# Router logits from un-normalised features, a first gather in pieces, another order of expert groups, and a second layer norm by column blocks

## The reference

```python
h = layer_norm(DEEPNORM_ALPHA * x + merged @ w_o, ln1_g, ln1_b)
# hierarchical_moe(h): top-1 of 4 groups, then top-2 of its 8 experts
grp_logits = tok @ w_gr + b_gr
exp_logits = (tok @ w_er + b_er).reshape(-1, N_GROUPS, EXPERTS_PER_GROUP)
...
hid = silu(tok @ w_g[e]) * (tok @ w_u[e])      # 32 experts, 2048 -> 256 -> 2048
out = (hid * combine) @ w_d[e]
ple = sigmoid(h @ w_pg) * (p @ w_pp)           # w_pg 2048 x 2048, w_pp 256 x 2048
x_new = layer_norm(DEEPNORM_ALPHA * h + moe + ple, ln2_g, ln2_b)
```

## Time and profile before

| | us |
|---|---|
| median of 3 runs (lowest, highest) | 1623.52 (1616.81, 1628.93) |
| the profiled execution, its time | 1617.29 |
| the profiled execution, its span | 1615.5 |
| busy: PE, PEld, DVE, ACT, POOL | 1435.6, 1082.9, 758.8, 333.8, 96.9 |
| moved by DMA, mean rate | 353.23 MB, 219 GB/s |

### The profile page before, as it was taken

How to read it: one execution, slowest core, us unless ns; L and a number is a source line. 1 busy time by engine, 2 the same in 40 slices (tenths; PEclk the granted TensorE clock), 3 DMA queues, 4 the chain that set the end, 5 groups by cost and what they waited for, 6 DMA issues and landing times.

```text
span 1615.5 us, 21195 instructions
## 1 busy us (share of the span) xinstructions
PE 1435.6 (89%) x8725; PEld 1082.9 (67%) x8725; DVE 758.8 (47%) x1499; ACT 333.8 (21%) x468; POOL 96.9 (6%) x94
## 2 busy tenths in 40 slices
PE   6969999999999999998999989888999698789671
PEld 4968998777788678768999975563465265346220
DVE  3749777888864246315565554302213142120237
ACT  3413331000010010015344442131202101200102
POOL 2730000000010100000010020000000000000002
PEclk9979999999999799979999996799999899999976
DMA  8424444333333433424554470389999999999991
GB/s 220 151 92 164 142 148 133 109 109 109 108 121 118 130 100 110 136 98 137 180 188 169 170 295 27 137 337 359 392 405 409 409 403 372 409 406 405 409 380 55
DMA packets 139039, 353.23 MB, mean 219 GB/s; under 512 B 20644, under 2 KB 21724, under 8 KB 138416
## 3 DMA queue, kind: packets, MB, share of 16 engines
q1 hardware_dynamic: 135944, 341.99, 57.8%
q0 software_dynamic: 2992, 9.81, 2.1%
HBM read 344.60 MB, written 7.18 MB: 218 GB/s over the span
## 4 chain that ended last, share of the span: by engine, by line
PE 75%; DMA 12%; DVE 7%; issue 2%; ACT 2%; SPq 1%; DVEq 0%; ACTq 0%
PE bank L520 72%; DMA mslot<-in_w_exp_up 6%; DMA mslot<-in_w_exp_down 5%; DVE lo L1574 1%; DVE atok L2327 1%; ACT hi L1303 1%; PE bank L535 1%; PE bank L792 1%; DMA stS<-in_state_hgrn 1%; SPq L1158 1%; DMA ident<-in_consts 1%; ACT htok L1422 0%; DVE stS L1896 0%; DVE stats L2408 0%; PE bank L907 0%
## 5 line engine op out<-in xcount | busy, mean ns | idle before, releaser
L520 PE MATMUL bank<-XT,raw 128*128 128x264 f32 x1280 | 309.1, 402 | 0.0
L520 PEld LDWEIGHTS bank<-XT,raw 128*128 128x128 f32 x1280 | 250.3, 198 | 47.3 <-issue 3.2
L1574 DVE TENSOR_TENSOR lo<-raw,hi 128x2048 fp32r<-128x2048 f32 x68 | 157.3, 2314 | 132.7 <-ACT hi L1303 132.6
L520 PE MATMUL bank<-mslot,Xg 128*32 128x512 f32 (+1 forms) x1024 | 146.6, 664 | 41.1 <-DMA mslot<-in_w_exp_up 40.0
L1303 ACT ACTIVATE hi<-raw 128x2048 fp32r<-128x2048 f32 x68 | 130.1, 1914 | 233.3 <-PE bank L520 229.8
L520 PE MATMUL bank<-XH,hi 128*128 128x264 f32 x512 | 148.9, 291 | 7.4 <-DVE lo L1574 6.2
L520 PE MATMUL bank<-XL,hi 128*128 128x264 f32 x512 | 147.3, 288 | 0.0
L520 PE MATMUL bank<-XH,lo 128*128 128x264 f32 x512 | 146.3, 286 | 0.0
L520 PEld LDWEIGHTS bank<-mslot,Xg 128*32 128x32 f32 (+1 forms) x1024 | 40.6, 123 | 124.5 <-issue 123.6
L520 PE MATMUL bank<-HT,mslot 128*128 128x264 f32 x512 | 116.3, 387 | 0.0
L520 PE MATMUL bank<-mslot,hidT 128*32 128x512 f32 (+1 forms) x512 | 79.6, 719 | 33.2 <-DMA mslot<-in_w_exp_down 33.2
(11 more groups left out here) (389 smaller groups left out, 2268.4 us busy)
## 6 DMA issues: line engine op xcount, KB each, us to landing
raw<-in_w_in SPq DMA_DIRECT2D x72, 1024.0 KB, 5.1
mslot<-in_w_exp_gate SPq DMA_DIRECT2D x128, 512.0 KB, 11.2
mslot<-in_w_exp_up SPq DMA_DIRECT2D x128, 512.0 KB, 12.8
mslot<-in_w_exp_down SPq DMA_DIRECT2D x64, 1024.0 KB, 14.0
raw<-in_w_out SPq DMA_DIRECT2D x16, 1024.0 KB, 5.0
mslot<-in_w_ple_gate SPq DMA_DIRECT2D x16, 1024.0 KB, 14.3
raw<-in_w_branch_b SPq DMA_DIRECT2D x8, 1024.0 KB, 5.0
raw<-in_w_branch_a SPq DMA_DIRECT2D x8, 1024.0 KB, 5.0
```

The costliest lines, as they stand in the source:

```text
L520: return nc.tensor.matmul(out, w, x, start=start, stop=stop)
L1574: v.tensor_tensor(lo[:, n % RD, :], raw[:, n % RD, :], hi[:, s % RH, :].bitcast(F32), ALU.subtract).then_inc(lo_done, 1)
```

## The change

- **Router.** `wrr` is loaded with feature k*128+p on partition p (before p*16+k). Its gain is multiplied in while the last dense product runs (at `N_O`, on DVE), and `raw_logits` multiplies it with the un-normalised `XT`, four tiles after each `to_tokens`. Scale and shift are applied to the 36 logits per token, with the column sums `wall`. `h_features` and `logits` go.
- **First gather.** It takes `htok` itself in float32 (three products per tile instead of five split ones) and stands in pieces ahead of the first three steps of the first group (`FIRST_GATHER`). The two slices of the gate product ahead of the selection go, so all ten slots are loaded with expert weights; the split of `htok` comes after the first gather.
- **HT** is made from `XT` by DVE and ACT during the first two groups, with the scalars spread over partitions by PE (`spread_scalars`).
- **Plan.** Fixed group, four quads, two pairs, two quads; the gate product moves to groups 2, 3, 4 and 7, `rest` to group 8. Feature order of the gate weights as for `wrr`.
- **Second layer norm.** Statistics of a column block follow its scatter in the last group; gain and bias come as two 8 KB loads which `norm_rows` spreads with eight products on PE; final scaling writes `ynorm` in halves of 1024 columns, and the stores stand ahead of the test of `flag`. The last group's down weights come in three pieces of 2, 1 and 1 column blocks (`pieces`).

The reading of the flag and the jump have left their place behind the last adding, and the statistics of a block follow its adding, two rows a block. The diff, cut to its core:

```diff
-PLANS = [[list(range(FIXED))] + PAIRS[2:4] + QUADS] + [PAIRS] * 4
+PLANS = [[list(range(FIXED))] + QUADS[:4] + PAIRS[2:4] + QUADS[4:]] + [PAIRS] * 4
...
-PLE_AT = {0: 0, 3: 1, 5: 2, 7: 3}
-PLE_AHEAD = (0, 1)
-REST_AT = 5
+PLE_AT = {2: 0, 3: 1, 4: 2, 7: 3}
+REST_AT = 8
+FIRST_GATHER = {0: (0, 1, 2), 1: (3, 4), 2: (5, 6, 7), 3: ()}
...
+        def pieces(rnd, g):
+            return ((0, 2), (2, 3), (3, 4)) if (rnd, g) == (0, len(PLANS[0]) - 1) else ((0, 2), (2, 4))
...
+            def raw_logits(j):
+                if j == 0:
+                    pe.wait_ge(w_gained, 1)
+                    b = side("wall")
+                    mm(b[:, 0:72], ones[:, :], wsum[:, :, :].rearrange("p i n -> p (i n)"), True, True).then_inc(
+                        misc_ready, 1)
+                for J in range(4 * j, 4 * j + 4):
+                    last = mm(bank[7][0:36, 0:NT], wrr[:, J], XT[:, J], J == 0, J == KD - 1)
+                if j == 3:
+                    last.then_inc(logT_done, 1)
...
+                    raw_logits(j)
...
-            def h_features(k):
-                b = side(("ht", k))
...
+                if cb == 0 and kq == 0:
+                    pe.wait_ge(ht_done, KD)
...
-            for kq in PLE_AHEAD:
-                ple_gate(0, kq)
...
+            def first_gather(u):
+                b = side(("ga", 0, 0, u))
+                if u == 0:
+                    pe.wait_ge(norm_act, 3)
+                    pe.wait_ge(zeroed, 3)
+                    pe.wait_ge(sel_ready, 1)
+                sel = [selm[:, 0, 0, 0:128].bitcast(F32), selm[:, 0, 1, 0:128].bitcast(F32),
+                       sels[0:NB, 0, 0:128].bitcast(F32)]
+                for q in range(2):
+                    ks = slice((2 * u + q) * 128, (2 * u + q + 1) * 128)
+                    for tt, (t0, tn) in enumerate(TOK):
+                        last = mm(b[:, q * 256:q * 256 + 128], htok[0:tn, tt, ks], sel[tt], tt == 0, tt == 2)
+                last.then_inc(misc_ready, 1)
...
+            def spread_scalars():
+                pe.wait_ge(diag_ready, 1)
+                for i in range(2):
+                    b = side(("spread", i))
+                    for tt, (t0, tn) in enumerate(TOK):
+                        last = mm(b[:, t0:t0 + tn], ones[0:tn, :], diag[0:tn, i, t0:t0 + tn], True, True)
+                    last.then_inc(misc_ready, 1)
...
+                        for u in FIRST_GATHER[s]:
+                            first_gather(u)
+                        stored(("ga", 0, 0, 2 * s))
+                        stored(("ga", 0, 0, 2 * s + 1))
                     for i in range(ne):
...
                     turn(rnd, g)
+                if rnd == 0:
+                    norm_rows(0)
                 for nb in range(4):
                     scatter(rnd, groups - 2, nb)
...
+            def norm_rows(again):
+                pe.wait_ge(ln2_ld, 32)
+                for r in range(8):
+                    b = side(("row", again, r))
+                    mm(b[:, :], ident[0:8, r:r + 1].to_broadcast([8, 128]), ln2row[:, :], True, True).then_inc(
+                        misc_ready, 1)
...
-                                 t["w_ple_gate"][0].rearrange("(p k) n -> p k n", p=P)[
+                                 t["w_ple_gate"][0].rearrange("(k p) n -> p k n", p=P)[
...
+                            dst = mslot[c % RM][:, 0:1024 * (n1 - n0)]
+                            sp.dma_start(dst.rearrange("p (j d) -> p j d", j=2),
+                                         src[:, :, 512 * n0:512 * n1]).then_inc(m_land[c % RM], 16)
...
+                    if rnd == 0 and g == len(plan) - 1:
+                        sp.wait_ge(misc_ready, misc["ple", 3, 2][0] + 1)
+                        for i, n in enumerate(("ln2_gain", "ln2_bias")):
+                            sp.dma_start(ln2row[4 * i:4 * i + 4, :], t[n][0].rearrange("(r n) -> r n", r=4)).then_inc(
+                                ln2_ld, 16)
...
-                gate_up_done(sp, rnd, len(plan) - 1)
-                for i, n in enumerate(("ln2_gain", "ln2_bias")):
-                    sp.dma_start(ln2[:, i, :], t[n].to_broadcast([P, D])).then_inc(ln2_ld, 16)
-            ple_load(0, PLE_AHEAD)
...
+            def store_rows(again):
+                for tt, (t0, tn) in enumerate(TOK):
+                    dst = outs[0][0, t0:t0 + tn, :] if tt < 2 else outs[1].rearrange("b a d -> (b a) d")
+                    for half in range(2 if tt < 2 else 1):
+                        cs = slice(1024 * half, 1024 * (half + 1)) if tt < 2 else slice(0, D)
+                        if tt < 2 or again:
+                            sp.wait_ge(f_out, 4 * again + 2 * tt + half + 1 + (tt == 2))
+                        else:
+                            sp.wait_ge(f_small, 1)
...
+                pool.dma_start(wrr[:, :, 4:36],
+                               t["w_expert_router"][0].rearrange("(k p) g -> p k g", p=P)).then_inc(r_ld, 16)
...
+            pool.wait_ge(flag_ready, 1)
             for tt in range(3):
                 nc.gpsimd.memset(atok[:, tt, :], 0.0).then_inc(zeroed, 1)
...
+                        nc.scalar.activation(htok[0:tn, tt, :], htok[0:tn, tt, :], ACT.Identity,
+                                             bias=nmr[0:tn, tt:tt + 1],
                                              scale=rstd[0:tn, tt:tt + 1]).then_inc(norm_act, 1)
-            act.wait_ge(norm_dve, 1)
...
+            def norm_rows(again):
+                for r in range(8):
+                    b, read = side(("row", again, r))
+                    if r == 0:
+                        gate_up_done(act, *((4, len(PLANS[4]) - 1) if again else (0, len(PLANS[0]) - 1)))
+                    nc.scalar.activation(ln2[:, r // 4, (r % 4) * 512:(r % 4 + 1) * 512], b[:, :],
+                                         ACT.Copy).then_inc(read, 1)
...
                 for tt, (t0, tn) in enumerate(TOK):
-                    last = v.tensor_tensor(logit[0:tn, tt, :], b[0:tn, tt * 36:(tt + 1) * 36],
-                                           rbias[0:tn, :], ALU.add)
+                    link(v.scalar_tensor_tensor(out=logit[0:tn, tt, :], in0=wall[0:tn, 0, :],
+                                                scalar=nmr[0:tn, tt:tt + 1], in1=wall[0:tn, 1, :],
+                                                op0=ALU.mult, op1=ALU.add))
+                settle()
+                for tt, (t0, tn) in enumerate(TOK):
+                    last = v.scalar_tensor_tensor(out=logit[0:tn, tt, :], in0=b[0:tn, tt * 36:(tt + 1) * 36],
+                                                  scalar=rstd[0:tn, tt:tt + 1], in1=logit[0:tn, tt, :],
+                                                  op0=ALU.mult, op1=ALU.add)
                     if tt < 2:
                         link(last)
...
+                                         lnk[:, 1, :].unsqueeze(2).to_broadcast([P, KD, 36]), ALU.mult))
+                    settle()
+                    link(v.tensor_tensor(wrr[:, :, :], wrr[:, :, :],
+                                         lnk[:, 0, :].unsqueeze(2).to_broadcast([P, KD, 36]), ALU.mult))
+                    link(v.tensor_reduce(wsum[:, 1, :], wrb[:, :, :].rearrange("p k n -> p n k"), AX_X, ALU.add))
+                    settle()
+                    v.tensor_reduce(wsum[:, 0, :], wrr[:, :, :].rearrange("p k n -> p n k"), AX_X,
+                                    ALU.add).then_inc(w_gained, 1)
...
+                for i, scalar in enumerate((rstd, nmr)):
+                    for tt, (t0, tn) in enumerate(TOK):
+                        last = v.tensor_scalar(diag[0:tn, i, t0:t0 + tn], ident[0:tn, 0:tn], scalar[0:tn, tt:tt + 1],
+                                               None, ALU.mult)
+                last.then_inc(diag_ready, 1)
...
+            def h_lows():
+                dve.wait_ge(h_high, 3)
+                dve.wait_ge(misc_ready, misc["ga", 0, 0, 7][0] + 1)
+                v.tensor_tensor(hS[32:32 + NB], by_k(htok[0:NB, 2, :]), hS[0:NB].bitcast(F32),
+                                ALU.subtract).then_inc(split_done, 1)
+                for half in range(2):
+                    for tt in range(2):
+                        h_low(tt, half)
...
+            def features():
+                for i in range(2):
+                    side_read(dve, ("spread", i))
+                for half in range(2):
+                    x = XT[:, 8 * half:8 * half + 8, :]
+                    for i, op in enumerate((ALU.mult, ALU.add)):
+                        if i:
+                            dve.wait_ge(ht_mul, 2 * half + 1)
+                        v.tensor_tensor(x, x, spread_ln[:, i, :].unsqueeze(1).to_broadcast([P, 8, NT]),
+                                        op).then_inc(ht_mul, 1)
...
+            def row_statistics(nb):
+                for tt, (t0, tn) in enumerate(TOK):
+                    final_link(v.bn_stats(stats[0:tn, tt, nb, :], atok[0:tn, tt, nb * 512:(nb + 1) * 512]))
+            def last_give_back(g):
+                store(0, g, 0)
```

(35 more changed lines are left out.)

314 lines of the change are left out of this document (150 added, 164 removed).

## The result

The changed kernel takes 1609.8 us (median of 10 runs, 1602.66 to 1611.91), the kernel before in the same comparison 1622.8 us (10 runs, 1616.81 to 1628.93). The ratio is 0.9914, with a 95% interval of 0.9894 to 0.9934: 13 us faster, where 31.5 were forecast. The profiled execution took 1610.45 us with a span of 1608.6.

The account below looks back on a forecast made before the run. Weight DMA (210 MB) was taken to bound the time after the router, with the queue idle in the router. 41.4 - 2.8 - 15.4 = 23.2 us to the last landing plus 8.3 in the tail: 31.5 off 1623.5 gives 1592 us, range 1573 to 1609.

Parts of the forecast that it names:

- Tail: From the last landing to the end: 45.65 us shrinks to 37.3, 8.3 us won, bounds 5 and 12.
- Dense stage: Twelve raw-logit products among the dense blocks, partly in PE's idle time: +3.5 us, bounds 0 and 7.
- the ring: Dense stage: ring of three banks instead of four makes PE wait about 1 us in the first round.
- Router: First four slots come free at 990 us, 46.5 us earlier; net 41.4 with ten slots loaded instead of twelve.
- The stream: Expert and embedding weight loads after the router: loses 22.2 us against 19.4 before, 2.8 us given back.
- The hand walk: Both plans walked group by group, PE pieces 3% above rows, 2.56 us a slot: last landings 1563.4 before, 1524.8 new.
- They are balanced: Groups 2, 3 and 4, each with an embedding part: 73, 64 and 73 us of PE against 73 of DMA.
- Ahead of the last landing: Last two half-size down loads wait for slots the first down piece frees: 15.4 us given back, bounds 5 and 19.
- Rival 2: PE bounds the stream; at 8% instead of 3% the landing comes 17 us later: 1609 us (1602 to 1616), chance 0.15.
- Rival 1: Clock stays up and PE keeps ahead; landing 15 us earlier: 1576 us (1569 to 1583), chance 0.24.
- Rival 3: Slower than before: PE waits for weights, its clock drops, stacked groups start at the lower level: 1633 us, chance 0.04.
- Rival 4: Router step not early: ACT's queue or the smaller ring delays the first copies 15 to 20 us: 1610 us, chance 0.07.

Follow-up runs that it names:

- Run 1: Changed kernel with the 8-row tile's last gain and bias step done by DVE instead of ACT and POOL: 1602.88 us, ratio 0.9885.
- run 4: Changed kernel with all sixteen products of raw logits behind the dense stage's last transposes, none between its blocks: 1606.93 us, ratio 0.9909.
- run 2: Changed kernel with the last group's down weights in two halves again (8 loads, not 12): 1603.35 us, ratio 0.9882.
- run 3: Changed kernel with gain and bias rows spread by two DMA copies instead of PE's products and ACT's copies: 1599.43 us, ratio 0.9862.
- run 5: Changed kernel with two units of the first gather, not three, ahead of the first gate/up step: 1606.62 us, ratio 0.9895.
- all together: Changed kernel plus small tile on DVE, gain/bias rows by DMA, first down piece before scatter 7, two units first, embedding part in group 1: 1583.9 us, ratio 0.9751.

## Why the prediction was wrong, point by point

The sign was right and so was most of the mechanism, but one of the two gains, the tail's, did not come at all. The size was 2.4 times too large: 13 us instead of 31.5, and 1609.8 lies just outside the range, which ended at 1609. From MH: 31.5 forecast, minus 5.9 in the router, minus 4.7 in the stream and ahead of the landing, minus 9.8 in the tail, is 11.1.

- **Tail (forecast +8.3, bounds 5 and 12; measured -1.5). This is the step that failed**: "DVE's eight halves at 2.29 / 2 = 1.15 to 1.2 us", beside "two rows of 4.5 on POOL". The durations were nearly right (1.27, 4.70), but they were laid side by side, and the two engines exclude each other. DVE lost 10.87 - 2.44 = 8.4 us, and its other halves took 0.4 us more than forecast. Another 1.6 us are DVE's row after the landing, with the scalars ready 22.9 us behind it instead of 21.3. From DVE's last instruction to the end are 6.0 us, where the forecast had 6.5 (37.3 - 30.8). That is 9.8 to 9.9 in all. Nor was POOL's small tile last, as forecast: it was done at 1596.75, DVE's last half at 1602.62. Run 1 shows the cause. The lower bound of 5 was wrong in kind: no row excluded a contention, and two rows of before (3.47 and 1.25 us for one column) showed it.
- **Dense stage (3.5; measured 3.4).** Right in sum, for a partly wrong reason: the ring adds nothing, the products leave 3.4 of 5.7 us (run 4).
- **Router (first load 46.5 us earlier; measured 40.6).** Scale and shift came 5.7 us after the last addition, where 6.0 were forecast, and the choice as forecast. Counts, ranks and selection took 5.2 us instead of 3.8; three units 11.2 instead of 7.7; the first step 4.9 instead of 4.4. The step that failed here is "a pass took 16.62 / 80 = 0.208 us": these passes took 11.2 / 36 = 0.31. The clock isn't the reason, as both stretches lay at the lower level. A window over the 80 passes of before, and two of them from PE's timeline:

```profile
1013.41:1030.03 16.62, 16.61 (x80) 16.42 (x80) 8.05 (x21) 5.65 (x14) 0.00 (x0) 0.52 0.06 22
```
```profile
1014.89 0.41 PE L520 MATMUL bank<-selm,hH 128*128 128x128 f32 x1
1015.10 0.41 PE L520 MATMUL bank<-selm,hL 128*128 128x128 f32 x1
```

A pass over a split part, 128 columns, started every 0.21 us at the lower level and every 0.11 at the higher (1013.54 to 1013.65 us). The four passes over `htok` itself took 1.15 us at the lower level and 0.64 at the higher, 0.29 and 0.16 each, and the two over the samples 0.72 and 0.42, 0.36 and 0.21 each. So the new product is dearer per pass at either level, 0.31 and 0.18 us on average where the prediction had 0.208 and 0.12; that it is so because it runs in plain float32, the other on rounded parts, is likely but no run tries it. Its price had to come from rows of its own kind; the three units cost 3.5 of the 5.9 us by it. For the counts it is the clock: PE took 3.3 us (978.67 to 981.93) at 0.50, where the 2 us of the forecast came from a stretch at 1.00.
- **The stream (-2.8).** Only with the wait for slots at the end taken away can it be read: run 2 landed at about 684.2 from MH, where 712.9 less the 35.5 us of head start (40.6 - 5.1) would be 677.4, so 6.8 us were given back. The hand walk had PE's pieces 3% above their rows everywhere; it lacked a first group at clock 0.88 without a gap in PE, and the losses after groups 2 and 4. "They are balanced" (73 us against 73) was true only of the sums; that a late start of a group then stays, with nothing to spare behind it, is argued, not shown by a run of its own. Its "4.5 us from a free slot to the first data" is in no row: in the trace of before the load issued at 1002.62 us, 1 MB in two halves, had landed whole by 1007.4, 4.8 us later.
- **Ahead of the last landing (-15.4).** 700.3 - 684.2 = 16.1. Right, by the steps named: the slots came free 24.3 us after down(7), where 24 were forecast. The two ends were each too long and cancel in part, which is luck: from there to the landing 5.3 us instead of 7, and without the wait (run 2) 13.1 from down(7) to the landing instead of 16.5. But it isn't all path: run 2 gives 6.3 us back, run 3 8.7, since PE's chain is next in line.
- **Slot and chain mechanics** (SP's queue standing still to the first step, four slots free at once, two loads waiting for the down piece) were as described.
- **Rivals.** Rival 2 (PE bounds the stream) gave nearly the measured time, 1609, but by another mixture: the pieces at full clock stood at their rows (3.64 and 7.28 us), and the stream lost 4 us more than forecast, not 17. Rival 1's clock did not come, though runs 4 and 5 show how near it was. Rivals 3 and 4 did not come. That a rival's number fits is no evidence for it; the table above is.
- **Sums.** Three are off by less than 1 us: 36 passes of 0.208 are 7.5, not 7.7; the terms up to the scalars in the tail make 21.05, not 21.3; and 24 + 7 - 16.5 is 14.5, not 15.4. None of them changes the outcome.

The range was too narrow on the slow side because no term in it could turn against the change in the tail.

## What to carry to other kernels

When an edit puts work of DVE and POOL side by side, don't price them by their durations alone: look in the trace for a DVE instruction with two SBUF operands that is much longer than its twins, and see whether it ends with one of POOL's. When a landing moves, ask what on the compute engines ends next; here 16 us at the landing were 6 at the end. And where two traces are compared, count from a common instruction ahead of the edit: here the start before it wandered by 6.6 us, half as much as the effect. And a product of a new kind is not priced from another's rows: here a pass took 0.31 us instead of 0.21 at the same clock.

## What the runs showed of the hardware

- DVE and POOL: 8.4 us lost in the changed kernel, POOL's second instruction stretched from 4.50 to 5.35 us in turn, and nothing of it left once POOL was idle (runs 1 and all together).
- The granted clock at the start of the first group depends on details of PE's row just before it: with one unit (3.7 us) less ahead of the first step it stayed at 1.00, with it it fell (near 1011 us in the changed kernel) and the passes went back from 0.71 to 1.22 us. It was so in every trace of each form. Why the drop is avoided isn't settled: the same happened with 5.7 us of products moved behind the last addition (run 4), and what the two have in common was not tried.
- Passes of 128 columns over float32 tokens (`selm,htok`) started every 0.29 us at the lower and 0.16 us at the higher level, those over the rounded parts of before every 0.21 and 0.11.
- A step of 32 passes takes 3.64 us at full clock. Behind waits for weights of 2.6 to 5.0 us such steps took 5.34 us in the changed kernel (starts 1505.66 to 1526.55 us, granted clock 0.68), and 6.04 to 6.14 us behind waits of 4.2 to 5.2 in the one before (0.59 in the longest). But two steps of before behind waits of 3.3 us took 3.64, at 1.00, so the wait alone doesn't decide it.
